# Second block's attention: a new order of the filling products, of VectorE's steps and of one PSUM ring

## The chip, the cores and the metric

One core of a Trainium2 chip runs the whole program as one launch. The metric is the device time of that launch in microseconds (us), as the median of three runs. A profiled execution of the same program gives the trace.

## What is computed

256 tokens of width 1024 pass two layers of a first block (mixer, memory attention, convolutional feed-forward) and then one layer of a second block. Only the first part of the second block is touched:

```python
xn = rmsnorm(x, norm_mix)
(u_rnn, u_gate, q, k_c, v_c, k_s, v_s, k_w, v_w, g_nsa, g_a, g_b) = jnp.split(xn @ w_in, cuts, axis=-1)
h_a = rg_lru(causal_depthwise_conv(u_rnn, conv_w, conv_b), gate_a_w, ..., lru_lambda)
y_a = h_a * jax.nn.gelu(u_gate, approximate=True)
y_b = nsa_mixer(q, k_c, v_c, k_s, v_s, k_w, v_w, g_nsa, ...)
merged = jax.nn.sigmoid(g_a) * (y_a @ proj_a) + jax.nn.sigmoid(g_b) * (y_b @ proj_b)
```

`rg_lru` is a gated linear recurrence on 1344 features: two block-diagonal gate products (4 blocks of 336), a tanh-built sigmoid of each, a decay `exp(...)`, and a scan over the tokens. `nsa_mixer` holds, for 16 heads of 64, attention over 15 compressed blocks, and two softmax attentions over the tokens (selected and window keys), each with a relative bias and a gate.

## The kernel before

**Products.** The weights arrive in one stream of pieces. A piece that is not "native" is split into a high and a low half: ScalarE casts the high half (`highs`, L991, the cast at L998), VectorE subtracts it for the low half (`lows_due`, L1499, at L1503), and TensorE adds three products (high-high, high-low, low-high) in `run` (L478). `features` (L484) makes one 128- or 112-column product of the layer's input over 8 row tiles: 24 matmuls of 256 columns. Native pieces are used as they come.

**The ring of pieces.** SyncE loads groups into a ring of NR = 4 places. Two neighbouring pieces of the same shape share a group, a native piece has one for itself (`grouped`, L176). A place is loaded again when TensorE has used the group four before. ScalarE and VectorE split up to LA = 3 pieces ahead of the one in hand, in the order of the stream, and wait for a piece that hasn't landed.

**PSUM.** Eight banks form two rings of four (L271): M for the streamed products, A for transposes, scores and attention values. `take` gives the next bank of a ring and waits for the engine that last emptied it.

**The stage around the change.** Twelve products `ur` (the recurrence's input, 112 features each), twelve `ug` (its gate, through `gelu_gate`, L812 and L1312, ScalarE's Gelu_apprx_tanh at L1315), and 24 small gate products (`lru`: three native matmuls each, recorded as six, then Tanh at L1377). After a `ur` product ScalarE copies it to `up`, and VectorE makes the depthwise convolution from four instructions (L2002, three times L2007). A decay step is Tanh, Exp and Square on ScalarE (L1349, L1351, L1353) and two VectorE instructions (L1987, L1991). In the order of TensorE's program: the twelve `ug` lie around the compression of keys and values (`phi`, its window sums `phi_sums` on VectorE, L1929, then `hid`, `cmp`), the transposes of queries and keys follow, and then the attention: for each of two query tiles i a compressed part (`csc`, `cpT`, `cpv`) and eight units un of four heads. Each unit issues scores (L947), the transposes of the unit before (L581), two steps of the list `lru_steps` as filling (`lru_next(2)`), and the values of the unit before (L934). Tile 0 has one block of 128 keys, tile 1 two. `lru_steps` (L437) is walked by TensorE, ScalarE and VectorE alike: 12 convolutions, 24 gate products, 3 decays; 38 of its 39 steps lie in the attention.

On VectorE a unit runs: copy of half the transposed probabilities (L2084, tile 1 only), maxima with the bias (L2069, L2072), after ScalarE's four exponentials (L1415) the reciprocals (L2075, L2077), then the two filling steps, then `finish`: the values of the unit before, scaled, out of PSUM (L2097). GpSimd adds them up (L2330). The attention's values lie in ring A, so that a unit of tile 1 takes five banks of a ring of four. After the attention the sixteen gate products `g2` follow, which need a Sqrt over the recurrence's factors first (L1437) on ScalarE and then Tanh (L1445).

Of the kernel before, what the change touches and what calls it, by code (L numbers as in the profile page):

```python
# [231 lines left out]
def build(nc, wstream, specs_out, cst_d, rel_d, par_d, par2_d, x_d, xT_d, memT_d, lnp_d, scr_d, out_d, layout):  # L232
    with ExitStack() as ctx:
# [230 lines left out]
        def tensor(e):  # L464
# [350 lines left out]
            for n in range(3):  # L815
                gelu_gate(n)
# [4 lines left out]
            gelu_gate(3)  # L821
            for c in range(2):
# [9 lines left out]
                gelu_gate(4 + 2 * c)  # L832
                gelu_gate(5 + 2 * c)
# [9 lines left out]
            for n in range(8, 12):  # L843
                gelu_gate(n)
# [17 lines left out]
            lru_todo = iter(lru_steps)  # L862

            def lru_next(n):
                for _ in range(n):
                    kind, m, *how = next(lru_todo, ("none", 0))
                    if kind == "conv":
                        features(("ur", m), W2, 8, 128, RW, span(UR + m * RP, RP), X, [], act, "ur", m)
                    if kind == "lru":
                        wi, jt = how  # L870
                        if jt == 0:
                            lru_w[:] = piece(("lru", m, wi), RP, 3, 336, (("GATE", ("gate_a_w_2", "gate_x_w_2")[wi], m), None, None),
                                             native=True)
                        x, (wW,) = lru_w
                        b = M.take(w, ("lru", m, wi, jt), act, "lru", m, wi, jt)
                        w.wait_ge(*landed(x))
                        w.wait_ge(vec, "xc", 3 * m + 2)
                        run(b[0:RP, 0:T], [(wW[:, k, jt * RP:(jt + 1) * RP], xc[0:RP, 3 * m + k, :]) for k in range(3)]
                            ).then_inc(*product.done("lru", m, wi, jt))
                        if jt == 2:  # L880
                            product.also("used", x)

            lru_w = [0, 0]
            for i in range(2):
# [102 lines left out]
        def scalar(e):  # L987
# [329 lines left out]
            for i in range(2):  # L1317
                for j in range(2):
                    w.wait_ge(act, "q2", j, i)
                    w.wait_ge(act, "kb", j, i)  # L1320
                if i:
                    w.wait_ge(vec, "qss", 0)
                e.activation(S[:, 0:1536], qb[:, i, :], ACT.Square).then_inc(*act.done("qsq", i))
                gelu_gate(i)
            gelu_gate(2)
            gelu_gate(3)
            for c in range(2):
                highs_of("phi", c)
                w.wait_ge(product, "phi", c)
                e.activation(ytmp[0:60, 256 * c:256 * c + 256], M["phi", c][0:60, 0:256],  # L1330
                             ACT.Gelu_apprx_tanh).then_inc(*act.done("phi", c))
                gelu_gate(4 + 2 * c)
                gelu_gate(5 + 2 * c)
                if c == 0:
                    w.wait_ge(cross, "cmp", 0)
                    e.activation(kc2[:, 0:64], A["cmp", 0][0:60, 0:64], ACT.Square, accum_out=kss).then_inc(*act.done("kss"))
            for n in range(8, 12):
                gelu_gate(n)
            for i in range(2):
                for h in range(2):  # L1340
                    w.wait_ge(cross, "q2T", i, h)
                    e.copy(q2[:, 4 * h:4 * h + 4, i * 128:(i + 1) * 128],
                           A["q2T", i, h][:, :].rearrange("p (k t) -> p k t", t=128)).then_inc(*act.done("q2T", i, h))

# [11 lines left out]
            for c in range(2):  # L1356
                for b in range(4):
                    w.wait_ge(stage_in[c][b])
            tmp_free = [(cross, "phT", 1)]
            lru_todo = iter(lru_steps)  # L1360

            def lru_next(n):
                for _ in range(n):
                    kind, m, *how = next(lru_todo, ("none", 0))
                    if kind == "conv":
# [17 lines left out]

            for i in range(2):
# [110 lines left out]
        def vector(e):  # L1495
# [420 lines left out]
            e.tensor_scalar(gq8, p2("qn"), 0.125, None, ALU.mult).then_inc(*vec.done("gq8"))  # L1916
            for i in range(2):
# [5 lines left out]
                lows_for("ug", i)  # L1923
            lows_for("ug", 2)
# [45 lines left out]
            for n in range(8, 12):  # L1970
                lows_for("ug", n)
# [10 lines left out]

            def decayed(m, n):
                tl, a2 = ytmp[0:RP, 0:256], ytmp[0:RP, 256:512]
                w.wait_ge(act, "lru", m // 3, 1, m % 3)
                w.wait_ge(vec, "xc", m)
                e.scalar_tensor_tensor(ia[0:RP, m, :], ia[0:RP, m, :], 1.0, xc[0:RP, m, :], ALU.add, ALU.mult).then_inc(*vec.done("ix", m))  # L1987
                w.wait_ge(act, "a2", m)
                w.wait_ge(vec, "ix", m)
                w.wait_ge(product, "lru", n, 1, 2)  # L1990
                e.scalar_tensor_tensor(xc[0:RP, m, :], a2, 1.0, tl, ALU.add, ALU.mult).then_inc(*vec.done("mult", m))  # L1991

            lru_todo = iter(lru_steps)

            def lru_next(n):
                for _ in range(n):
                    kind, m, *how = next(lru_todo, ("none", 0))
                    if kind == "conv":
                        lows_for("ur", m)
                        o = xc[0:RP, m, :]  # L2000
                        w.wait_ge(act, "ur", m)
                        e.tensor_scalar(o, up[0:RP, m, 3:259], cw2[:, m, 3:4], cb2[:, m:m + 1], ALU.mult,  # L2002
                                        ALU.add).then_inc(*vec.done("xc", m))
                        w.wait_ge(pool, "pad")
                        for k in range(3):
                            w.wait_ge(vec, "xc", m)
                            e.scalar_tensor_tensor(o, up[0:RP, m, k:k + T], cw2[:, m, k:k + 1], o, ALU.mult,  # L2007
                                                   ALU.add).then_inc(*vec.done("xc", m))
# [504 lines left out]
```

## Time and profile before

| | us |
|---|---|
| median of 3 runs (lowest, highest) | 1663.39 (1661.22, 1664.31) |
| profiled execution | 1660.03 |
| its span in the trace | 1658.2 |
| TensorE busy in the span | 1557.0 |
| VectorE, ScalarE, GpSimd busy | 1028.6, 800.3, 246.6 |
| from the first `ug` to the first score of tile 0 | 1109.9 to 1165.7 |
| attention, tile 0 | 1165.7 to 1242.3 |
| attention, tile 1 | 1242.3 to 1326.9 |
| four `g2` products | 1326.9 to 1339.5 |

Times within the trace count from the span's start. Busy time of TensorE includes the modelled end of each matmul, so that the time from one start to the next is the surer measure of what a piece of work takes. "Idle before" in a row of the timeline is the engine's wait before that row, and the arrow names who ended it.

### The profile page before, as it was taken

The page shows a single profiled execution, that of the slowest core. Times are in us where ns is not written, and L with a number is a line of the kernel's source. Part 1 is how long each engine was busy: PE and PEld are TensorE (multiplying, and loading weights), DVE is VectorE, ACT ScalarE, POOL GpSimd, SP SyncE. Part 2 cuts the span into 40 slices and gives each one's busy share as a digit, 9 for nine tenths or more (in the row PEclk, how much of TensorE's full clock was granted, in tenths as well). Part 3 has the DMA queues.
Part 4 walks back from the last instruction along what each step waited for, and adds up shares of the span by engine and source line. Part 5 has one row for each costly group of instructions (what it writes and reads, how often), then busy time and mean ns, then how long its engine had stood idle before and what let it go on. Part 6 is the DMA issues. An engine that isn't in the chain of part 4 may idle for free.

```text
span 1658.2 us, 25362 instructions
## 1 busy us (share of the span) xinstructions
PE 1557.0 (94%) x10403; PEld 1401.7 (85%) x10403; DVE 1028.6 (62%) x1704; ACT 800.3 (48%) x1435; POOL 246.6 (15%) x225
## 2 busy tenths in 40 slices
PE   8999999898998999989989999899988799989999
PEld 6899888798986889988789986697876699979987
DVE  5764585675855575577677865445655486646643
ACT  4545445364642455444356652453445564435532
POOL 2300131211202130032031101003010041100000
PEclk9999999899999999999999999899999899989999
DMA  8523355359554533255345555455211244535543
GB/s 314 222 102 115 103 216 174 119 178 218 190 208 152 203 123 111 88 190 181 128 160 190 182 192 176 152 184 187 90 45 48 77 153 148 202 107 189 188 178 127
DMA packets 41027, 261.33 MB, mean 158 GB/s; under 512 B 4512, under 2 KB 5152, under 8 KB 14672
## 3 DMA queue, kind: packets, MB, share of 16 engines
q1 hardware_dynamic: 35600, 238.44, 41.5%
q0 software_dynamic: 2944, 15.69, 3.7%
q10 hardware_dynamic: 2368, 5.58, 0.9%
q8 instruction: 82, 1.34, 0.3%
q14 instruction: 33, 0.27, 0.0%
HBM read 254.98 MB, written 4.19 MB: 156 GB/s over the span
## 4 chain that ended last, share of the span: by engine, by line
PE 75%; DVE 11%; ACT 5%; issue 3%; DMA 3%; POOL 2%; ACTq 0%; DVEq 0%; POOLq 0%; SPq 0%
PE ps L478 67%; PE ps L581 3%; DMA raw<-d_wst 2%; DVE lows L1503 2%; POOL sm L2189 1%; PE ps L662 1%; ACT wh L998 1%; ACT S L1415 1%; DVE ar L2007 1%; DVE sm L1536 1%; DVE xs L1533 1%; PE ps L683 1%; DVE S L2069 1%; PE ps L577 1%; PE ps L701 0%
## 5 line engine op out<-in xcount | busy, mean ns | idle before, releaser
L1503 DVE TENSOR_TENSOR lows<-raw,wh 128x1024 fp32r<-128x1024 f32 (+3 forms) x473 | 546.1, 1174 | 261.3 <-ACT wh L998 258.5
L478 PE MATMUL ps<-xTr,wh 128*128 128x256 f32 (+2 forms) x3664 | 674.1, 286 | 17.0 <-DVE S L1833 7.5
L478 PEld LDWEIGHTS ps<-xTr,wh 128*128 128x128 f32 (+2 forms) x3664 | 574.7, 192 | 22.3 <-issue 14.2
L998 ACT CAST wh<-raw 128x1024 fp32r<-128x1024 f32 (+3 forms) x473 | 455.6, 989 | 176.1 <-DMA raw<-d_wst 164.4
L478 PE MATMUL ps<-xTr,lows 128*128 128x256 f32 (+2 forms) x1832 | 522.0, 285 | 0.0
L478 PEld LDWEIGHTS ps<-xTr,lows 128*128 128x128 f32 (+2 forms) x1832 | 352.4, 192 | 0.0
L478 PE MATMUL ps<-wh,arR 128*128 128x512 f32 x928 | 296.4, 398 | 4.1 <-DVE ar L1653 4.1
L478 PEld LDWEIGHTS ps<-wh,arR 128*128 128x128 f32 x928 | 175.1, 189 | 48.1 <-DVE ar L1653 5.8
L478 PE MATMUL ps<-lows,arR 128*128 128x512 f32 x464 | 184.1, 397 | 0.0
L478 PE MATMUL ps<-arR,wh 128*128 128x256 f32 (+1 forms) x832 | 147.2, 280 | 2.2 <-DVE lows L1503 2.2
L478 PE MATMUL ps<-wh,xTr 128*128 128x512 f32 x384 | 125.0, 405 | 12.2 <-DVE xTr L1522 6.7
L478 PEld LDWEIGHTS ps<-arR,wh 128*128 128x128 f32 (+1 forms) x832 | 126.7, 188 | 2.8 <-issue 2.6
L478 PE MATMUL ps<-arR,lows 128*128 128x256 f32 (+1 forms) x416 | 116.0, 279 | 0.0
L478 PEld LDWEIGHTS ps<-lows,arR 128*128 128x128 f32 x464 | 87.6, 189 | 20.6
L478 PEld LDWEIGHTS ps<-wh,xTr 128*128 128x128 f32 x384 | 75.6, 197 | 30.8 <-DVE xTr L1522 7.1
L2189 POOL TENSOR_TENSOR sm<-sm,cst 128x1 f32<-128x1 f32 (+3 forms) x27 | 42.3, 1566 | 384.4 <-DVE sm L1541 235.5
L478 PEld LDWEIGHTS ps<-arR,lows 128*128 128x128 f32 (+1 forms) x416 | 78.2, 188 | 0.0
L478 PE MATMUL ps<-lows,xTr 128*128 128x512 f32 x192 | 77.5, 404 | 0.0
L2275 POOL TENSOR_TENSOR S<-S 128x256 f32<-128x256 f32 x44 | 42.0, 955 | 222.8 <-ACT S L1225 201.0
L1243 ACT ACTIVATE S<-ps,ar 128x256 f32<-128x256 f32 x88 | 49.4, 562 | 51.1 <-PE ps L478 51.1
L2263 POOL TENSOR_TENSOR ar<-ar 128x256 f32<-128x256 f32 x32 | 31.9, 998 | 233.3 <-DVE ar L1653 233.1
L1415 ACT ACTIVATE S<-S,sm 128x128 f32<-128x128 f32 (+1 forms) x64 | 28.3, 443 | 56.6 <-DVE sm L2072 56.5
(265 smaller groups left out, 1554.0 us busy)
## 6 DMA issues: line engine op xcount, KB each, us to landing
raw<-d_wst SPq DMA_DIRECT2D x196, 1024.0 KB, 4.8
raw<-d_wst SPq DMA_DIRECT2D x24, 512.0 KB, 3.5
raw<-d_wst SPq DMA_DIRECT2D x12, 896.0 KB, 4.6
raw<-d_wst SPq DMA_DIRECT2D x8, 672.0 KB, 4.6
ar<-d_lnp POOLq DMA_DIRECT2D x5, 1024.0 KB, 5.2
raw<-d_wst SPq DMA_DIRECT2D x8, 441.0 KB, 3.4
d_scr<-PT POOLq DMA_DIRECT2D x1, 3072.0 KB, 37.0
ar<-d_par POOLq DMA_DIRECT2D x2, 1192.0 KB, 9.6
```

Of the source, the lines that this page charges most:

```text
L478: op = e.matmul(out, s, m, start=start and i == 0, stop=stop and i == len(pairs) - 1)
L577: e.matmul(b[:, :], ident, cst("wmask"), start=True, stop=True)
L581: op = e.transpose(o, x, ident[0:x.shape[0], 0:x.shape[0]])
L662: op = e.matmul(b[:, h * 64:(h + 1) * 64], PTv[:, hold + h, k, :], va[:, k, v:v + 64], start=(k == 0), stop=(k == 1))
L683: op = e.matmul(bv[:, k, :], qT[br][lo:lo + 64, 2 * hh + k, i * 128:(i + 1) * 128], kT[br][lo:lo + 64, :], start=True, stop=True)
L998: e.copy(high_of(m), raw_of(m)).then_inc(*high.done(m))
L1243: e.activation(hc[:, s, :], M["up", l, m][:, 0:T], ACT.Identity, bias=cb[:, m:m + 1], scale=ck[:, m, 1:2]).then_inc(*act.done("h", l, m))
L1415: op = e.activation(Sv[:, hold + h, 0:nk], Sv[:, hold + h, 0:nk], ACT.Exp, bias=nb[:, h:h + 1], scale=1.0, accum_out=su[:, h:h + 1])
L1503: e.tensor_tensor(low_of(m), raw_of(m), high_of(m).bitcast(F32), ALU.subtract).then_inc(*low.done(m))
L2189: return e.tensor_tensor(dst, src, mhalf[0:p, 0:n], ALU.pow)
L2263: e.tensor_tensor(merged[:, d, :], merged[:, d, :], gates[:, gate_at[n] + d, :], ALU.add).then_inc(*pool.done("merged", l, n, d))
L2275: e.tensor_tensor(hc[:, s, :], hc[:, s, :], hc[:, s + 1, :], ALU.mult).then_inc(*pool.done("z", l, n))
```

## The change

- `lru_steps` now holds 51 steps: the twelve `ug` products are steps of it too. Six convolutions and three `ug` lie ahead of the attention where twelve `ug` lay. In tile 0 the other six convolutions alternate with gate products, in tile 1 nine `ug` alternate with gate products, one of each in a unit. The attention still takes 38 steps; four (one gate product with its decay, three decays) are left behind it, where one decay was.
- VectorE's convolution of step n is issued in step n + 1.
- VectorE's `finish(un - 1)` stands ahead of the two filling steps of unit un.
- The attention's values are written to ring M.
- Behind the attention ScalarE and VectorE split the pieces of the first `g2` products ahead of the steps that are left.
- GpSimd's clearing of `up`'s first columns stands ahead of the load of the bias table.

```diff
@@ lru_steps
-        lru_steps = [("conv", n) for n in range(RN)]
-        lru_steps += [("lru", n, wi, jt) for n in range(4) for wi in range(2) for jt in range(3)]
-        lru_steps += [("decay", 9 + k) for k in range(3)]
+        gate_steps = iter([("lru", n, wi, jt) for n in range(4) for wi in range(2) for jt in range(3)])
+        lru_steps = [("conv", 0), ("conv", 1), ("ug", 0), ("conv", 2), ("conv", 3), ("ug", 1), ("conv", 4), ("conv", 5), ("ug", 2)]
+        lru_steps += [("conv", 6), ("conv", 7)]
+        for n in range(8, RN):
+            lru_steps += [next(gate_steps), ("conv", n), next(gate_steps), next(gate_steps)]
+        lru_steps += [next(gate_steps)]
+        for n in range(3, RN):
+            lru_steps += [("ug", n), next(gate_steps)]
+        lru_steps += [*gate_steps, *(("decay", 9 + k) for k in range(3))]
@@ TensorE
-            for n in range(3):
-                gelu_gate(n)
...
+            lru_next(3)
             b = A.take(w, ("ng",), vec, "ng")
...
-            gelu_gate(3)
+            lru_next(1)
             for c in range(2):
...
-                gelu_gate(4 + 2 * c)
-                gelu_gate(5 + 2 * c)
+                lru_next(2)
...
-            for n in range(8, 12):
-                gelu_gate(n)
+            lru_next(1)
...
                 def finish(un):
-                    b = A.take(w, ("pv2", i, un), vec, "o2", i, un)
+                    b = M.take(w, ("pv2", i, un), vec, "o2", i, un)
@@ ScalarE (gelu_gate and lru_next as on TensorE)
+                    if kind == "ug":
+                        gelu_gate(m)
...
+            for n in range(3):
+                highs_of("g2", 0, n)
             lru_next(60)
@@ VectorE
+            def lru_next(n):
+                for _ in range(n):
+                    kind, m, *how = next(lru_todo, ("none", 0))
+                    if kind == "ug":
+                        lows_for("ug", m)
+                    if kind == "conv":
+                        lows_for("ur", m)
+                    if conv_due[0] is not None:
+                        convolved(conv_due[0])
+                    conv_due[0] = m if kind == "conv" else None
...
                 e.tensor_scalar(ve[i][:, 24:48], ve[i][:, 0:24], 1.0 / 64, 1e-6, ALU.mult, ALU.add).then_inc(*vec.done("qv", i))
-                lows_for("ug", i)
-            lows_for("ug", 2)
+                lru_next(1)
+            lru_next(1)
...
             phi_sums(0)
-            lows_for("ug", 3)
+            lru_next(1)
             q_scaled(0)
             for c in range(2):
                 lows_for("phi", c)
-                lows_for("ug", 4 + 2 * c)
+                lru_next(1)
                 if c == 0:
                     phi_sums(1)
-                lows_for("ug", 5 + 2 * c)
+                lru_next(1)
                 w.wait_ge(cross, "phT", c)
...
                     maxima(un)
-                    lru_next(2)
                     if un:
                         finish(un - 1)
+                    lru_next(2)
                 probs_copied(7)
+                finish(7)
                 lru_next(1)
-                finish(7)
...
+            for n in range(3):
+                lows_for("g2", 0, n)
             lru_next(60)
@@ GpSimd
             first_block_done()
+            e.memset(up[0:RP, :, 0:3], 0.0).then_inc(*pool.done("pad"))
...
-            e.memset(up[0:RP, :, 0:3], 0.0).then_inc(*pool.done("pad"))
```

## Rows read from the trace of the kernel before

**Rows 1.** Busy time by stage (length, engines, granted clock, DMA): tile 0, tile 1, then g2.

```profile
1165.69:1242.28 76.59, 67.60 (x527) 62.28 (x528) 48.69 (x165) 33.71 (x104) 5.82 (x8) 0.98 0.20 63
1242.28:1326.86 84.58, 67.64 (x397) 55.80 (x396) 39.62 (x140) 48.61 (x130) 5.82 (x8) 0.89 0.19 61
1326.86:1339.49 12.63, 12.63 (x97) 12.44 (x96) 7.17 (x12) 12.47 (x17) 0.74 (x1) 0.91 0.25 83
```

**Rows 2.** Waits of TensorE, both tiles: who ended them, us in total, times, longest.

```profile
PE ps L581 <- DVE ar L2097: 9.4, 5, 2.2
PE ps L934 <- DVE PT L2084: 4.5, 1, 4.5
```

**Rows 3.** Timeline of TensorE, tile 0: start, us, line, tiles, count, idle before.

```profile
1177.06 0.50 PE L478 MATMUL ps<-xTr,wh 128*112 128x256 f32 x2
...
1182.88 0.72 PE L947 MATMUL ps<-ar 64*128 64x128 f32 x8
1183.53 0.66 PE L581 MATMUL ps<-cst,S 128*128 128x128 f32 x4
...
1208.42 1.10 PE L934 MATMUL ps<-ar,PT 128*128 128x64 f32 x8 [0.79 <-DVE ar L2097]
...
1233.79 2.75 PE L478 MATMUL ps<-ar,raw 112*112 112x256 f32 x12
```

**Rows 4.** Timeline of TensorE, tile 1: one unit, then the end.

```profile
1259.15 2.00 PE L934 MATMUL ps<-ar,PT 128*128 128x64 f32 x16
1261.08 1.14 PE L947 MATMUL ps<-ar 64*128 64x256 f32 x8
1262.15 0.66 PE L581 MATMUL ps<-cst,S 128*128 128x128 f32 x4
1264.88 0.66 PE L581 MATMUL ps<-cst,S 128*128 128x128 f32 x4 [2.07 <-DVE ar L2097]
...
1319.86 3.64 PE L934 MATMUL ps<-ar,PT 128*128 128x64 f32 x16 [4.50 <-DVE PT L2084]
```

**Rows 5.** Timeline of ScalarE, one unit of tile 1.

```profile
1260.03 0.51 ACT L1415 ACTIVATE S<-S,sm 128x256 f32<-128x256 f32 x1 [1.83 <-DVE sm L2072]
...
1262.01 0.45 ACT L1377 ACTIVATE ar<-ps,sm 112x256 f32<-112x256 f32 x1
1262.36 0.59 ACT L1349 ACTIVATE ar<-ar,sm 112x256 f32<-112x256 f32 x1
...
1264.30 0.58 ACT L1404 COPY PT<-ps 128x512 f32<-128x512 f32 x1
```

**Rows 6.** Timeline of ScalarE: the first Gelu_apprx_tanh, and the first Exp after it.

```profile
1115.51 1.28 ACT L1315 ACT_TABLE_LOAD   x1
1116.81 0.39 ACT L1315 ACTIVATE ar<-ps 112x256 f32<-112x256 f32 x1
...
1169.44 1.28 ACT L1388 ACT_TABLE_LOAD   x1 [3.89 <-DVE S L2039]
```

**Rows 7.** The page's group of casts (count, busy, mean ns), and the loads of two pieces (KB, us to landing).

```profile
L998 ACT CAST wh<-raw 128x1024 fp32r<-128x1024 f32 (+3 forms) x473 | 455.6, 989 | 176.1 <-DMA raw<-d_wst 164.4
...
raw<-d_wst SPq DMA_DIRECT2D x2, 896.0 KB, 4.6
```

**Rows 8.** Timeline of VectorE: three quarters of a convolution, then copy and end of maxima.

```profile
1184.37 1.52 DVE L2007 SCALAR_TENSOR_TENSOR ar<-ar,par 112x256 f32<-112x256 f32 x3
...
1265.57 0.69 DVE L2084 COPY PT<-ps 128x512 f32<-128x512 f32 x1 [0.75 <-PE ps L581]
1267.67 0.17 DVE L2072 TENSOR_SCALAR sm<-sm 128x4 f32<-128x4 f32 x1
```

**Rows 9.** Timeline of TensorE at the first compression product.

```profile
1122.73 2.56 PE L478 MATMUL ps<-raw,S 128*60 128x256 f32 x11 [1.03 <-DVE S L1940]
```

**Rows 10.** Timeline of ScalarE behind the attention: Sqrt, first g2 Tanh.

```profile
1331.42 2.77 ACT L1437 ACTIVATE ar<-ar 112x3072 f32<-112x3072 f32 x1
...
1336.43 0.39 ACT L1445 ACTIVATE PT<-ps 128x256 f32<-128x256 f32 x1
```

More of the change, by code:

```diff
@@ L813, in gelu_gate @@
                 features(("ug", n), W2, 8, 128, RW, span(UG + n * RP, RP), X, [], act, "ug", n)
-            for n in range(3):
-                gelu_gate(n)
+            lru_w = [0, 0]
+            lru_todo = iter(lru_steps)
+            def lru_next(n):
[4 more added lines that the diff above has]
+                    if kind == "conv":
+                        features(("ur", m), W2, 8, 128, RW, span(UR + m * RP, RP), X, [], act, "ur", m)
+                    if kind == "lru":
+                        wi, jt = how
+                        if jt == 0:
+                            lru_w[:] = piece(("lru", m, wi), RP, 3, 336, (("GATE", ("gate_a_w_2", "gate_x_w_2")[wi], m), None, None),
+                                             native=True)
+                        x, (wW,) = lru_w
+                        b = M.take(w, ("lru", m, wi, jt), act, "lru", m, wi, jt)
+                        w.wait_ge(*landed(x))
+                        w.wait_ge(vec, "xc", 3 * m + 2)
+                        run(b[0:RP, 0:T], [(wW[:, k, jt * RP:(jt + 1) * RP], xc[0:RP, 3 * m + k, :]) for k in range(3)]
+                            ).then_inc(*product.done("lru", m, wi, jt))
+                        if jt == 2:
+                            product.also("used", x)
+            lru_next(3)
             b = A.take(w, ("ng",), vec, "ng")
@@ L860, in tensor @@
                        [qb[:, i, 1024 + k * 128:1024 + (k + 1) * 128] for k in range(4)])
[L862 to L883, printed above, removed]
             for i in range(2):
@@ L1315, in gelu_gate @@
                 e.activation(gg2[0:RP, n, :], M["ug", n][0:RP, 0:T], ACT.Gelu_apprx_tanh).then_inc(*act.done("ug", n))
[L1317 to L1343, printed above, removed]
             def decayed(m):
@@ L1354, in decayed @@
                 tmp_free[0] = (vec, "mult", m)
[L1356 to L1359, printed above, removed]
             lru_todo = iter(lru_steps)
@@ L1364, in lru_next @@
                     kind, m, *how = next(lru_todo, ("none", 0))
+                    if kind == "ug":
+                        gelu_gate(m)
                     if kind == "conv":
@@ L1382, in lru_next @@
                         decayed(m)
+            for i in range(2):
+                for j in range(2):
+                    w.wait_ge(act, "q2", j, i)
+                    w.wait_ge(act, "kb", j, i)
+                if i:
+                    w.wait_ge(vec, "qss", 0)
+                e.activation(S[:, 0:1536], qb[:, i, :], ACT.Square).then_inc(*act.done("qsq", i))
+                lru_next(1)
+            lru_next(2)
+            for c in range(2):
+                highs_of("phi", c)
+                w.wait_ge(product, "phi", c)
+                e.activation(ytmp[0:60, 256 * c:256 * c + 256], M["phi", c][0:60, 0:256],
+                             ACT.Gelu_apprx_tanh).then_inc(*act.done("phi", c))
+                lru_next(2)
+                if c == 0:
+                    w.wait_ge(cross, "cmp", 0)
+                    e.activation(kc2[:, 0:64], A["cmp", 0][0:60, 0:64], ACT.Square, accum_out=kss).then_inc(*act.done("kss"))
+            lru_next(1)
+            for i in range(2):
+                for h in range(2):
+                    w.wait_ge(cross, "q2T", i, h)
+                    e.copy(q2[:, 4 * h:4 * h + 4, i * 128:(i + 1) * 128],
+                           A["q2T", i, h][:, :].rearrange("p (k t) -> p k t", t=128)).then_inc(*act.done("q2T", i, h))
+            for c in range(2):
+                for b in range(4):
+                    w.wait_ge(stage_in[c][b])
+            tmp_free = [(cross, "phT", 1)]
             for i in range(2):
@@ L1969, in vector @@
                     q_scaled(1)
-            for n in range(8, 12):
-                lows_for("ug", n)
+            lru_next(1)
             w.wait_ge(cross, "kcT")
@@ L1981, in vector @@
                               A["k2T", i][:, :].rearrange("p (w f t) -> p w f t", w=2, t=128)).then_inc(*vec.done("k2T", i))
[L1983 to L2008, printed above, removed]
-                    if kind == "lru":
-                        wi, jt = how
-                        if jt == 0:
-                            lows_for("lru", m, wi)
-                        if late_at(m, wi, jt):
-                            decayed(late_of(m, wi, jt), m - 1)
-                    if kind == "decay":
-                        decayed(m, 3)
             for i in range(2):
```

39 lines of the change are left out of this document (38 added, 1 removed).

## Prediction

> **What bounds the kernel now.** The page comes first: TensorE is busy for 1557.0 of 1658.2 us, so most of the program has nothing to give, and what can be won lies where TensorE pauses. The busy time by stage shows where that is: in tile 0 it works 67.6 of 76.6 us, in tile 1 67.6 of 84.6, there at a mean granted clock of 0.89 [rows 1]. The waits name what it stands for. The largest sum is the transposes that wait for VectorE's `finish`, 9.4 us in five times, then the values at the end that wait for VectorE's copy, 4.5 [rows 2]. The timelines show how. In tile 1 a unit takes five banks of ring A; the second transpose needs the bank of the values two units back, and VectorE empties it only behind its filling steps [rows 4]. TensorE has little filling there: two gate products of 1.4 [rows 3]. In tile 0 filling is plenty, but the values wait 0.79 for the same `finish` [rows 3].
>
> **Unit prices.** Start to start, a big product (`ur` or `ug`) costs 2.9 us (two in 5.82), a gate product 1.3 to 1.4; in tile 0 scores 0.65, transposes some 0.4, values 1.0 [rows 3]; in tile 1 scores 1.07, transposes 0.9, values 1.9 [rows 4]. On ScalarE four exponentials cost 2.0, a Tanh 0.35, a decay 1.6 (1.94 with the next Tanh), a copy 0.6 [rows 5], a cast 0.9 [rows 7]. On VectorE copy and maxima take 2.3, a convolution 1.9 (its last three instructions are 1.52) [rows 8].
>
> **The work that moves.** No product is added or dropped. Ahead of the attention 12 `ug` become 9 products, so 3 x 2.9 = 8.7 us leave that stage. Tile 0 gives up 6 of 12 big products and gains 6 gate products: 17.4 - 7.8 = 9.6 leave it. Tile 1 has 9 big ones more and 7 gate products fewer, +17.0; one gate product (+1.3) falls behind the attention. The sum is nought; only pauses count.
>
> **Ahead of the attention.** VectorE now does two convolutions (3.8) before the window sums for which the first compression product waits; that product already waits 1.03 for them [rows 9]. One ScalarE table load fewer ahead of its second Square gives 0.6 back, so TensorE arrives at the same time and waits 4.3: +3.2. Likewise a convolution stands ahead of `hid` in both halves: +1.8 and +1.1. The last convolutions lie beside `ug` 2. From -8.7 this leaves **-2.4**; below that it can't fall under -8.7, above it reaches +1 if the pause lowers the clock.
>
> **Tile 0.** With `finish` ahead of the filling and the values in ring M, the waits for VectorE go. A unit with a convolution is 0.65 + 0.4 + 1.0 + 2.9 + 1.3 = 6.2 us of TensorE, one with two gate products 4.6. VectorE needs about 4.6 and 5.5 for the two, as the convolution is put off into the second: 10.1 beside 10.8, so TensorE sets the pace until unit 6. There the first decays come, and ScalarE, which splits ahead, stands for the load of the next `ug` pieces: 1.1 and 2.0 us of pauses. The last values wait 1.4 for a copy behind a decay, the final transposes 1.4 for GpSimd as before. Added up from the first score product: 61.8 instead of 76.6, **-14.8**; if VectorE stays late as now, only the moved 9.6.
>
> **Tile 1: what ScalarE pays.** TensorE's unit becomes 1.07 + 0.9 + 2.9 + 1.3 + 1.9 = 7.9 to 8.1. But each `ug` is a Gelu_apprx_tanh between exponentials. In the trace such a change of function has a table load in front: 1.28, and 1.30 from its start to the activation, on the way to Gelu, and another at the next Exp [rows 6]. Nine `ug` in tile 1 make 18 loads, 23.4 us of ScalarE. A unit is then 2.0 + 0.9 + 1.3 + 0.3 + 0.35 + 0.6 + 1.3 = 6.8 without and 8.4 with a decay, and behind a decay the next exponentials wait for VectorE's last decay instruction, copy and maxima (2.6 instead of the 0.6 of the copy beside it). Two units make 17.1 against TensorE's 15.8: ScalarE is what is late next. The rule of the Trainium skill, ScalarE: Activation LUTs, Table sets: the hidden batching unit, says to batch activations by table set, and speaks against this order; the trace has the 1.30 to price it. Its section What ACT_TABLE_LOAD costs adds a drain to 2.66 us a switch, which would put the sum some 20 us higher; the activation 0.02 behind the load shows no such drain [rows 6].
>
> **Tile 1: the loads of the weights.** `lru_steps` puts the pairs u6-u7, u9-u10 and the first `g2` pair four places of the ring behind a gate piece that TensorE finishes in the second filling step of units 0, 3 and 6. ScalarE splits the first of each pair in the first step of the same unit, so it waits there until that product is done and the load has landed, 4.6 us [rows 7]. Queued behind it are the Gelu, the Tanh and the copy for which the values wait. Walked through from the stage's start, the exponentials of units 0, 1, 3, 5, 7 begin at 13.4, 23.4, 40.5, 63.5 and 80.2. After the last come two casts, two loads, Gelu, Tanh, decay and copy, 9.2 to 9.7, and the values start at 89.9; from there to the end I take the old length, 1319.86 to 1326.86 = 7.0 [rows 1, 4]. That is 96.9 instead of 84.6: **+12.3**. Bounds: 82 if TensorE sets the pace; 105 if the clock falls as in [rows 1].
>
> **Behind the attention.** The first four `g2` products take the four banks of ring M; the fifth needs the first Tanh. Now that Tanh ends at 1336.8, 10.0 behind the end of tile 1, and the products take 12.6 [rows 1, 10]: nothing waits. Now three casts (2.8), a Tanh (0.4) and three more decays with VectorE's answer between them (6.5) stand ahead of Sqrt, less the cast that stood there: 18.4. TensorE has 1.3 + 12 of work: +**5.8** on its path, up to +8 with a low clock, 0 if the decays overlap.
>
> **Cheap edits.** GpSimd's clearing moves past one load on its own queue, and its cover is the 60 us until the first use; uncovered it would cost under 1 us. The bank of the values in ring M is emptied by `finish` a unit before it is needed: nothing. Were that late, the next product would wait.
>
> **Sum.** -2.4 - 14.8 + 12.3 + 5.8 = +0.9. The pauses of 4 to 5 us ahead of the first compression product and at the fifth `g2` product can lower the clock to 1.2 GHz for a few us, as the transition after the 4.50 wait did, where values take 3.64 instead of 1.9 [rows 4]: +1 to +2. I take +2. The profiled execution was 1660.0 and its span 1658.2, and 3.4 lies between it and the median 1663.4; the sum is made against the first, so the median comes to 1665.5.
>
> **Rivals.** *ScalarE isn't late* (faster). It waits 1.83 ahead of the exponentials in [rows 5]; if loads fall into such waits and the pieces land earlier, tile 1 goes at TensorE's 8 a unit and ends at about 82: 15 less, 1650.5. Against it: a load behind the last Gelu still stands ahead of a decay's Exp. Chance 0.31. *The clock* (slower). If each pause of 2 to 3 us in tile 1 is followed by a unit at 1.2 GHz, as 0.89 suggests [rows 1], a unit grows by up to 4; it decides once three units run at the lower level. Three such units, and 2 ahead of the attention: +14, 1678. Chance 0.20. *The change doesn't do what it says*: VectorE is still late for the maxima in tile 0, and only the 9.6 comes: +5, 1671. Chance 0.10. *The drain of the skill's page*: 1685, chance 0.02; no row bears it out.
>
> **How the numbers follow.** The forecast, -4 to +7 around 1665.5, has 0.37. A measurement of this kernel can tell about 0.2%, 3.3 us. Faster: 0.28 of the first rival and 0.06 of the forecast, 0.34. Same: 0.20 of the forecast, 0.03 each of the first rival and the third, 0.26. Slower: 0.11, 0.20, 0.07, 0.02, together 0.40. The range reaches from the first rival's 1650 to the clock's 1678.
>
> **What would show it.** Right: 18 loads more on ScalarE between the ends of tile 0 and tile 1, casts there that wait for a load of weights, tile 0 near 62 us with no transposes waiting for `finish`, a wait of some 4 us ahead of the fifth `g2` product. Wrong: ScalarE idle ahead of the exponentials of tile 1, units there at 8 us, or Gelu without loads.

## The result, and the profile after

The changed kernel takes 1680.97 us in the median of four runs (1677.73 to 1684.64), against 1663.36 in four runs before: a ratio of 1.0116, 95% interval 1.0095 to 1.0137. The forecast was 1665.5 with a range of 1649 to 1678, so the time lies above the range.

The profiled execution of the changed kernel took 1682.51 and its span is 1680.7, 22.5 longer than before. 5.3 of that lies in the first 1110 us, where both kernels do the same: the first `ur` product starts at 1115.13, and the first `ug` before at 1109.86. Over the profiled executions of this study that point lies anywhere between 1109.9 and 1115.5, so what follows compares stages and not ends. The busy time of the changed kernel by stage (length, then TensorE, its weight loads, VectorE, ScalarE, GpSimd, the granted clock, DMA share, GB/s): ahead of the attention, tile 0, tile 1, and to the fifth `g2` product.

```profile
1115.13:1174.52 59.39, 50.99 (x321) 41.20 (x320) 38.01 (x68) 19.67 (x32) 16.34 (x7) 0.89 0.38 128
1174.52:1238.27 63.75, 57.32 (x418) 51.33 (x419) 40.30 (x145) 37.17 (x111) 8.56 (x8) 0.98 0.25 80
1238.27:1342.71 104.44, 86.92 (x570) 77.47 (x570) 42.48 (x134) 68.53 (x137) 5.92 (x8) 0.88 0.19 66
1342.71:1361.61 18.90, 13.99 (x102) 13.13 (x101) 10.49 (x20) 16.98 (x24) 0.34 (x1) 0.86 0.50 167
```

Beside [rows 1], and 55.8 (1109.86 to 1165.69) for the first stage before: +3.6, -12.8, +19.9, +6.3. Where the change took work away (the first stage) it is longer, and the clock there is 0.89. The largest waits of TensorE over all four stages (engine, tile, line, who ended it: us in total, times, longest):

```profile
PE ps L939 <- DVE PT L2097: 10.9, 3, 5.6
PE ps L484 <- ACT PT L1451: 4.9, 1, 4.9
PE ps L484 <- DVE ar L2010: 4.1, 2, 2.7
PE ps L484 <- DVE S L1989: 3.9, 1, 3.9
```

The transposes that waited for `finish` [rows 2] are gone; all five of those waits lay in tile 1. In tile 0 of the kernel before only values waited for `finish`, 2.8 in three times, and they do no longer:

```profile
PE ps L934 <- DVE ar L2097: 2.8, 3, 1.3
```

In place of the transposes the values of tile 1 wait for VectorE's copy of the probabilities (L2097). Ahead of each of the three copies in VectorE's queue stands the last instruction of a decay (L1931), and that waits for ScalarE's Square (L1330), by 1.8, 3.5 and 1.7. The second of them:

```profile
1295.22 0.43 DVE L1931 SCALAR_TENSOR_TENSOR ar<-ar 112x256 f32<-112x256 f32 x1 [3.48 <-ACT ar L1330]
1295.57 0.68 DVE L2097 COPY PT<-ps 128x512 f32<-128x512 f32 x1
```

The fifth `g2` product waits for a Tanh, the compression for `hid` (L2010) and for the window sums (L1989). Those two waits, and two later places, in the timeline of TensorE:

```profile
1130.88 10.00 PE L484 MATMUL ps<-raw,S 128*60 128x256 f32 x32 [3.91 <-DVE S L1989]
...
1149.64 0.43 PE L484 MATMUL ps<-par,ar 128*60 128x64 f32 x4 [2.67 <-DVE ar L2010]
...
1238.27 3.51 PE L900 MATMUL ps<-ar 128*128 128x60 f32 x16
...
1335.71 3.65 PE L939 MATMUL ps<-ar,PT 128*128 128x64 f32 x16 [5.55 <-DVE PT L2097]
```

The first compression product takes 10.0 for its 32 matmuls, where at the full clock it takes 7.09 (shown under e8_short); the granted clock of that stretch is 0.71 of 2.4 GHz:

```profile
1130.88:1140.88 10.00, 10.00 (x33) 5.48 (x33) 9.16 (x16) 0.00 (x0) 3.41 (x3) 0.71 0.25 88
```

What stands ahead of the window sums is two convolutions on VectorE, 3.8 us, as forecast:

```profile
1124.92 0.41 DVE L1936 TENSOR_SCALAR ar<-ar,par 112x256 f32<-112x256 f32 x1
1125.43 1.53 DVE L1941 SCALAR_TENSOR_TENSOR ar<-ar,par 112x256 f32<-112x256 f32 x3
1126.88 0.41 DVE L1936 TENSOR_SCALAR ar<-ar,par 112x256 f32<-112x256 f32 x1
1127.32 1.53 DVE L1941 SCALAR_TENSOR_TENSOR ar<-ar,par 112x256 f32<-112x256 f32 x3
...
1128.93 1.80 DVE L1989 TENSOR_TENSOR S<-PT,par 128x120 f32<-128x120 f32 x8
```

And tile 1 on ScalarE, unit 0: the exponentials start, then a cast waits 3.25 for weights that haven't landed, and around the Gelu stand two loads of tables, 1.28 each:

```profile
1254.97 0.51 ACT L1419 ACTIVATE S<-S,sm 128x256 f32<-128x256 f32 x1 [3.27 <-DVE sm L2085]
...
1260.30 0.94 ACT L1003 CAST wh<-raw 128x896 fp32r<-128x896 f32 x1 [3.25 <-DMA raw<-d_wst]
1261.25 1.28 ACT L1320 ACT_TABLE_LOAD   x1
1262.55 0.38 ACT L1320 ACTIVATE ar<-ps 112x256 f32<-112x256 f32 x1
...
1263.79 1.28 ACT L1419 ACT_TABLE_LOAD   x1
1265.08 0.51 ACT L1419 ACTIVATE S<-S,sm 128x256 f32<-128x256 f32 x1
```

Over tile 1 the groups by line count 9, 5 and 4 loads, the 18 of the forecast, and the waits of ScalarE hold the three landings:

```profile
L1320 ACT ACT_TABLE_LOAD x9 | 11.5, 1283 | 0.2
L1328 ACT ACT_TABLE_LOAD x5 | 6.4, 1283 | 0.1
L1419 ACT ACT_TABLE_LOAD x4 | 5.1, 1283 | 0.1
```
```profile
ACT wh L1003 <- DMA raw<-d_wst: 10.0, 3, 4.4
```

### The profile page after: what moved, and what is told of

It reads as the page before. It is cut to its first block and busy times, and to the rows that moved or that the text cites. A ratio compares the mean times of both kernels' runs of the same rounds, so it can differ in the third digit from the quotient of the medians.

```text
span 1680.7 us, 25388 instructions
## 1 busy us (share of the span) xinstructions
PE 1571.1 (93%) x10403; PEld 1414.7 (84%) x10403; DVE 1032.0 (61%) x1704; ACT 825.0 (49%) x1453; POOL 248.3 (15%) x225
## 5 line engine op out<-in xcount | busy, mean ns | idle before, releaser
L484 PEld LDWEIGHTS ps<-xTr,wh 128*128 128x128 f32 (+2 forms) x3664 | 580.2, 194 | 27.3 <-issue 14.5
L1839 DVE SCALAR_TENSOR_TENSOR S<-ps,ar,S 128x255 f32<-128x255 f32 x88 | 42.1, 479 | 11.6 <-ACT S L1248 11.6
```

The costliest lines, as they stand in the source:

```text
L484: op = e.matmul(out, s, m, start=start and i == 0, stop=stop and i == len(pairs) - 1)
L1839: e.scalar_tensor_tensor(h[:, 1:T], b[:, 0:T - 1], ck[:, m, 0:1], h[:, 1:T], ALU.mult, ALU.add).then_inc(*vec.done("conv0", l, m))
```

## Experiments

All start from the changed kernel. The theories: **P**, a pause of TensorE costs itself and the low clock behind it; **T**, the loads of tables set tile 1; **L**, so do the waits for landing weights; **B**, the decays left behind the attention hold up the first Tanh of `g2`. The table has the medians, the ratio to the kernel before with its interval, and the stages of the profiled execution: ahead (first 112-column product to first score product of the compressed part), tile 0 (to the same product of tile 1), tile 1 (to the first `g2` product) and behind (to the end). By these bounds tile 1 holds the last gate product too: 84.2 before, 106.4 after. The ratio is to the kernel before as it was run again beside each (medians 1660.7 to 1662.1), not to the first row's median. The changed kernel was not run again, so a difference of under 3 between two medians is not clear of this. The stages are those of one execution each: that of e8_short is the fastest of its seven, that of e4_mixed the slowest of its ten.

| kernel | median | ratio (95%) | ahead | tile 0 | tile 1 | behind |
|---|---|---|---|---|---|---|
| before | 1663.4 | | 55.8 | 76.6 | 84.2 | 331.7 |
| changed | 1681.0 | 1.0116 (1.0095 to 1.0137) | 59.4 | 63.8 | 106.4 | 336.0 |
| e1_tanh | 1666.9 | 1.0032 (1.0014 to 1.0051) | 59.3 | 63.8 | 91.9 | 336.7 |
| e2_conv_late | 1669.6 | 1.0049 (1.0034 to 1.0065) | 48.7 | 63.8 | 106.4 | 336.0 |
| e3_dummies | 1679.7 | 1.0121 (1.0101 to 1.0141) | 59.3 | 64.1 | 106.1 | 337.5 |
| e4_mixed | 1666.6 | 1.0028 (1.0014 to 1.0041) | 55.7 | 75.2 | 94.3 | 330.6 |
| e5_far2 | 1670.9 | 1.0053 (1.0036 to 1.0069) | 59.0 | 63.0 | 94.8 | 337.8 |
| e6_tail | 1678.8 | 1.0109 (1.0091 to 1.0127) | 59.0 | 63.8 | 106.6 | 335.5 |
| e7_batch | 1650.2 | 0.9930 (0.9911 to 0.9949) | 48.5 | 64.4 | 85.3 | 336.7 |
| e8_short | 1670.5 | 1.0046 (1.0029 to 1.0062) | 54.8 | 65.7 | 97.9 | 334.5 |
| e9_filled | 1639.9 | 0.9866 (0.9848 to 0.9883) | 48.4 | 62.2 | 79.6 | 334.3 |
| e10_ring_a | 1684.5 | 1.0137 (1.0120 to 1.0154) | 59.4 | 63.8 | 109.6 | 336.1 |
| e11_finish_late | 1680.7 | 1.0109 (1.0094 to 1.0124) | 59.6 | 63.5 | 107.2 | 336.6 |
| e12_both_undone | 1690.7 | 1.0174 (1.0158 to 1.0190) | 59.3 | 63.7 | 118.2 | 335.8 |

**The loads of tables (e1_tanh).**

```diff
-                e.activation(gg2[0:RP, n, :], M["ug", n][0:RP, 0:T], ACT.Gelu_apprx_tanh).then_inc(*act.done("ug", n))
+                e.activation(gg2[0:RP, n, :], M["ug", n][0:RP, 0:T], ACT.Gelu_apprx_tanh if n < 3 else ACT.Tanh).then_inc(*act.done("ug", n))
```

> The changed kernel with Tanh in place of Gelu_apprx_tanh in the nine `ug` steps of tile 1: a part of the computation is changed, so that ScalarE changes no function table there. Theory T (tables): 18 loads, 23 us of ScalarE, go away; the waits for landing weights (3.3, 4.4 and 2.4 us) stay; the other units go at TensorE's 8.0, and tile 1 falls from 104.2 to about 88, the whole from 1681 to about 1665. Rival W (weights): tile 1 is set by the landing of pieces in the ring, and the loads lie in those waits; tile 1 stays above 99, the whole above 1676. Rival C (clock alone): TensorE's clock sets the length, and tile 1 moves by under 3.

Tile 1 falls by 14.5 and nothing else moves. That is less than the 23.0 of the 18 loads. The rest shows in ScalarE's waits for the maxima ahead of its exponentials in tile 1, here in e1_tanh and then in the changed kernel: some 8 of the loads had lain in these.

```profile
ACT S L1419 <- DVE sm L2085: 19.6, 8, 3.3
```
```profile
ACT S L1419 <- DVE sm L2085: 11.6, 6, 3.3
```

The waits for landings stay in e1_tanh, so they are a cause of their own:

```profile
ACT wh L1003 <- DMA raw<-d_wst: 11.8, 3, 4.5
```

**The convolutions behind the window sums (e2_conv_late).** VectorE collects the convolutions of the six `ur` ahead of the attention in a list and makes them up later.

```diff
+                    if ahead[0]:
+                        put_off.extend([m] if kind == "conv" else [])
...
                 if c == 0:
                     phi_sums(1)
+                    made_up(2)
...
                     q_scaled(1)
+                    made_up(1)
             lru_next(1)
+            made_up(3)
+            ahead[0] = False
```

> The changed kernel, with VectorE's convolutions 0 to 5 moved behind the window sums: two behind the second sums, one behind the queries' scaling, three behind the last `ug` ahead of the attention. Theory P (the pauses pull the clock down): TensorE's waits ahead of the first compression product and the two small products fall from 3.9, 2.7 and 1.4 to 1.0, 0.8 and 0.4, the granted clock there rises from 0.7 to 1.0, and the stage falls from 59.4 to about 47.5, 6 of it from the waits and 6 from the clock: the whole comes to about 1669. Rival D (the waits only): the clock stays low for another reason, and 6 come back: 1675. Rival E: the convolutions now stand ahead of the masks and maxima at the start of tile 0, and what is won there is lost again: 1678 or more.

The stage falls by 10.7, to 48.7. The waits are 0.7 for the sums and 1.1 for `hid`, and the granted clock of the stage is 1.00, against 0.89:

```profile
PE ps L484 <- DVE ar L2019: 1.1, 2, 0.8
PE ps L484 <- DVE S L1997: 0.7, 1, 0.7
```
```profile
1112.29:1161.02 48.73, 45.05 (x321) 37.62 (x320) 37.78 (x68) 19.86 (x33) 14.46 (x7) 1.00 0.46 155
```

The waits named fell from 8.0 to 1.8, by 6.2, and a new one of 1.5 came at the transposes behind. The other 6 are clock. Rival D is out, and so is E: tile 0 didn't move.

**The clock by itself (e3_dummies, e8_short).** Only dummy products are added, so that TensorE is busy in its pauses.

```diff
+                if c == 0:
+                    warm(8)                      # e8_short: 4
                 for a in (0, 8):
...
+                if i:
+                    warm(12)                     # e8_short: 6
                 finish(7)
+                if not i:
+                    warm(4)                      # e8_short: 2
...
+                    if (v, n) == (0, 4):
+                        warm(11)                 # e8_short: 5
```

> The changed kernel with dummy products of TensorE in four of its pauses, each no longer than the pause: 8 ahead of the first compression product, 4 ahead of tile 0's last transposes, 12 ahead of tile 1's last values, 11 ahead of the fifth `g2` product. They work on constants and nothing reads them. Theory P: the waits' ends don't move, but the clock behind them stays at 2.4 GHz: first compression products 10.0 to 7.1, start of tile 1 (scores and `ug`) 8.2 to 4.7, last values 3.65 to 1.9; the whole falls by 7 to 11, to 1670 to 1674. Rival D: the clock is low for another reason, and the time stays at 1681 or rises by what the dummies outlast their pauses.

> The changed kernel with dummy products on TensorE in the same four pauses, but 4, 2, 6 and 5 of them, since each took 0.87 to 0.9 and the 8, 4, 12 and 11 outlasted their pauses (7.0 against 3.9 ahead of the first compression product). Theory P: they end inside the pauses, the clock behind stays at 2.4 GHz, and what the longer row gave back and lost at once is now kept: 2.9 at the first compression products, 3.5 at the start of tile 1, 1.8 at the last values: the whole falls by 6 to 9, to 1672 to 1675. Rival D: with dummies that leave a rest of the pause the clock falls all the same: 1679 or more.

e3_dummies misses its 1670 to 1674. I had taken a dummy at 0.44, from a row of such products with ten records; but each leaves two, and costs 0.87 to 0.9. With the eight of e3_dummies the first compression product starts 2.9 later after the start of its stage (18.7 instead of 15.8); it takes 7.12 instead of 10.0 and gives back the same 2.9. So the time of e3_dummies doesn't change, though its clock does:

```profile
1122.33 7.03 PE L583 MATMUL ps<-cst 128*128 128x512 f32 x16
1129.30 7.12 PE L484 MATMUL ps<-raw,S 128*60 128x256 f32 x32
```

With half of them the pause ends within 0.3 of where it did and the products behind are as fast. In e8_short, the same place and the start of tile 1:

```profile
1122.21 3.60 PE L583 MATMUL ps<-cst 128*128 128x512 f32 x8
1126.55 7.09 PE L484 MATMUL ps<-raw,S 128*60 128x256 f32 x32 [0.74 <-DVE S L1997]
...
1226.36 3.73 PE L583 MATMUL ps<-cst 128*128 128x512 f32 x4
...
1231.06 1.89 PE L902 MATMUL ps<-ar 128*128 128x60 f32 x16
```

The scores of the compressed part take 1.89 there instead of 3.51. Work that nobody reads makes the kernel 10.5 faster in the median (1681.0 to 1670.5). In the profiled execution the stages give 4.6 ahead, 8.5 in tile 1 and 1.5 behind, less 2.0 in tile 0. There the clock had already fallen in this execution: the two dummies take 3.73, about twice the price, and outlast their pause. Theory P holds, and this is what the low clock behind four pauses costs, less what the dummies cost themselves.

**Landing weights (e5_far2).**

```diff
-                highs_of("ug", n)
+                highs_of("ug", n, far=LA if n < 3 else 2)
-                            highs_of("lru", m, wi)
+                            highs_of("lru", m, wi, far=LA if m < 2 else 2)
```

and the same for VectorE's `lows_for`.

> The changed kernel, with ScalarE and VectorE splitting only two pieces ahead instead of three in tile 1, so that no piece is split in the step that frees its place. The loads of tables stay. Theory L (landing): ScalarE's waits of 3.3, 4.4 and 2.4 for weights go, tile 1 falls from 106.4 (first score product to first `g2`) to about 97, the whole to about 1671. Rival T2: the loads of tables alone set tile 1 and the waits had lain in ScalarE's slack: 103 or more, 1677 or more. Rival S: split later, the pieces are late for TensorE, which then waits for the low halves: no gain.

No wait for a DMA is left among ScalarE's in tile 1, and the stage falls by 11.6; a single wait of 1.4 of TensorE for low halves is what rival S brings. T and L are both true. The largest waits of ScalarE there are now those for VectorE's maxima and for the last transposes:

```profile
ACT S L1419 <- DVE sm L2085: 11.1, 5, 3.3
ACT arR L1432 <- PE ps L587: 6.8, 2, 6.5
```

**Another deal (e4_mixed).** The twelve `ug` stand ahead of the attention as before (the last `lru_next(1)` there is `lru_next(4)` on all three engines); c is an `ur`, g a gate product:

```diff
+        lru_steps = [("ug", n) for n in range(RN)]
+        for c in "cccc" "gcggcgggcgggcg" "g" "cg" "cgggcgcggggggg" "g":
+            lru_steps.append(next(conv_steps if c == "c" else gate_steps))
+        lru_steps += [("decay", 9 + k) for k in range(3)]
```

> Another deal of the same steps with the changed kernel's other edits: all twelve `ug` ahead of the attention as in the kernel before, eight `ur` and 11 gate products in tile 0, four `ur` and 13 gate products in tile 1, each gate product at least a unit behind the convolutions it needs; no Gelu and no convolution where it hurt. Theory T with P: ahead of the attention as before, 55.8; tile 0 and tile 1 together about 143 instead of 161 (before) and 168 (changed); two decays less behind the attention than in the changed kernel: the whole 1645 to 1650, faster than both. Rival V (the new places of `finish` and of the values give little, and tile 0 was shorter because products were taken out of it): 1658 or more.

At 1666.6 it is 17 slower than the upper end I expected and lies in rival V's range. That the new places of `finish` and of the values give little, as V has it, is shown below for tile 0 of the changed kernel's deal (e12_both_undone), not for this one. Tile 0 with its eight `ur` came to 75.2, and tile 1 to 94.3. The largest single piece is L again. In the step of the last `ur` ScalarE splits a `g2` piece whose place is only freed a unit later; it waits 8.39, VectorE's last convolution behind it, and a gate product 9.22 for that; the 14.5 behind this wait have a granted clock of 0.58. Two rows, of ScalarE and of TensorE:

```profile
1293.13 1.04 ACT L1001 CAST wh<-raw 128x1024 fp32r<-128x1024 f32 x1 [8.39 <-DMA raw<-d_wst]
```
```profile
1297.46 1.17 PE L482 MATMUL ps<-ar,raw 112*112 112x256 f32 x2 [9.22 <-DVE ar L1939]
```

So a deal without Gelu in the attention has the same trap; how this one does with two pieces ahead stays open.

**Behind the attention (e6_tail).**

```diff
-            lru_next(60)
...
+            lru_next(1)
+            for n in range(3):
+                g2_tanh(0, n)
+                lru_next(1)
```

> The changed kernel; on ScalarE the Tanh of the first three `g2` products stand between the four decays left behind the attention, ahead of Sqrt, instead of behind it. Theory B (behind the attention): the wait of 4.9 ahead of the fifth `g2` product goes, and with it 1 to 2 of low clock: the whole falls by 5 to 7, to about 1675. Rival R: Sqrt comes 1 to 2 later, the recurrence behind it is the next thing late, and the time stays at 1679 to 1683.

A miss: 2 instead of 5 to 7, and the 2 are not clear of the noise; the time is next to rival R's 1679, for another reason than rival R's. The wait for the Tanh is gone, but ScalarE, still at its decays and Sqrt, doesn't split the next pieces either, and a later `g2` product waits for them:

```profile
1360.47 0.77 PE L484 MATMUL ps<-xTr,wh 128*128 128x256 f32 x2 [3.60 <-DVE lows L1517]
```

**The parts together (e7_batch, e9_filled).** e7_batch joins e2_conv_late, e5_far2 and e6_tail, and takes the Gelu out of the attention without changing what is computed:

```diff
+                if n < 3:
+                    e.activation(gg2[0:RP, n, :], M["ug", n][0:RP, 0:T], ACT.Gelu_apprx_tanh).then_inc(*act.done("ug", n))
+                else:
+                    e.copy(gg2[0:RP, n, :], M["ug", n][0:RP, 0:T]).then_inc(*act.done("ugc", n))
...
             e.activation(qall, qall, ACT.Sqrt).then_inc(*act.done("sqrt"))
...
+            e.activation(gall, gall, ACT.Gelu_apprx_tanh).then_inc(*act.done("ug", 3))
```

> The changed kernel with four edits together: the convolutions behind the window sums (as measured: 10.7 less), the `ug` of the attention copied out of PSUM by ScalarE's Copy and nine of them given Gelu_apprx_tanh in one instruction behind Sqrt (no loads of tables in tile 1), two pieces ahead in tile 1, and the first `g2` Tanh between the decays. If the causes are what the theories T, P, L and B say they add up: 10.7 + 14.5 + 6 to 9 + 5 less than 1681, that is 1642 to 1645, faster than both kernels. Rival V: TensorE's 8 us a unit bind first, so that T and L don't add: 1650. Rival W: one more cause is hidden behind these: 1658 or more.

It is the first that beats the kernel before, but at rival V's 1650. T and L together give 21.1 in tile 1 and not 26.1: TensorE binds there first, as its units follow each other without a wait up to the last values, 7.96 from one set of scores to the next. The batch of Gelu was not run alone; with two pieces ahead tile 1 was 94.8 (e5_far2), and with the batch besides it is 85.3. And B's 5 don't come, as in e6_tail: a later `g2` product waits 4.6 for low halves. Two scores and the values between them, and TensorE's waits for low halves:

```profile
1253.46 1.14 PE L952 MATMUL ps<-ar 64*128 64x256 f32 x8
...
1259.59 1.90 PE L939 MATMUL ps<-ar,PT 128*128 128x64 f32 x16
1261.42 0.93 PE L952 MATMUL ps<-ar 64*128 64x256 f32 x6
```
```profile
PE ps L484 <- DVE lows L1525: 5.0, 2, 4.6
```

e9_filled adds to e7_batch what e6_tail, e7_batch and e8_short taught (`lows_for` on VectorE goes the same way as `highs_of`):

```diff
                 g2_tanh(0, n)
+                highs_of("g2", 0, n + 3)
...
+                if not i:
+                    warm(2)
                 probs_turned(7)
                 lru_next(1)
+                if i:
+                    warm(3)
                 finish(7)
+                warm(1)
```

> The four edits of the earlier run of this name's kind (convolutions late, Copy with Gelu in one batch, two pieces ahead, Tanh between the decays), and two more: ScalarE and VectorE split one more piece of `g2` behind each of those Tanh, and dummy products (0.87 each) stand in the pauses at the ends of the tiles: 2 and 1 in tile 0, 3 and 1 in tile 1. Theories B and P: the wait of 4.6 for low halves ahead of the seventh `g2` product goes, and the start of tile 1 (scores and `ug`, 8.1) goes at 2.4 GHz (4.7): 7 to 9 less than 1650, that is 1641 to 1643. Rival R: the recurrence or the weights behind take it back: 1647 or more.

1639.9, 1.3% under the kernel before, with a granted clock of 1.00 in all three stages. What the dummies and what the earlier splitting bring of the 10.3 from e7_batch was not run apart; the stages give 5.7 in tile 1, 2.2 in tile 0 and 2.4 behind.

```profile
1110.53:1158.94 48.41, 45.06 (x321) 37.64 (x320) 37.99 (x68) 19.63 (x32) 14.43 (x7) 1.00 0.46 156
1158.94:1221.12 62.18, 59.20 (x424) 51.34 (x425) 39.30 (x144) 35.98 (x110) 7.79 (x8) 1.00 0.25 82
1221.12:1300.71 79.59, 78.97 (x585) 69.88 (x583) 43.80 (x135) 45.61 (x122) 9.19 (x8) 1.00 0.24 87
```

**`finish` and the ring (e10_ring_a, e11_finish_late, e12_both_undone).**

```diff
-                    b = M.take(w, ("pv2", i, un), vec, "o2", i, un)      # e10, e12
+                    b = A.take(w, ("pv2", i, un), vec, "o2", i, un)
...
-                    if un:                                              # e11, e12
-                        finish(un - 1)
                     lru_next(2)
+                    if un:
+                        finish(un - 1)
```

> The changed kernel with the attention's values written to ring A again. Theory F (`finish` ahead of the filling is enough): tile 0, which needs four banks of ring A a unit, stays at 63.8; in tile 1, with five, the transposes wait for `finish` of the unit before, which comes later than the last exponentials only where VectorE is late: 0 to 3 more, the whole 1681 to 1684. Rival M (the ring is what freed the transposes): tile 0 rises by 4 to 6.

> The changed kernel with VectorE's `finish` behind the two filling steps again, the values in ring M. Theory F: in tile 0 the values' bank in ring M comes round again after three filling products, before `finish` has emptied it, and the filling waits: tile 0 rises by 3 to 6. Theory M (the ring alone is enough): tile 0 stays within 1 of 63.8; tile 1, set by ScalarE, doesn't move in either.

> The changed kernel with both undone: values in ring A and `finish` behind the filling steps, as in the kernel before; only the deal of the products stays. By the prediction's sum tile 0's 12.8 less is 9.6 of products moved out of it and the rest waits for `finish`: tile 0 comes to about 67, the transposes wait for `finish` again. Rival N: the waits in the kernel before came from twelve convolutions on VectorE, and with half of them and `put off` they don't come back: tile 0 stays at 64.

Tile 0 is 63.5 to 63.8 in all three: neither edit, nor both, does anything there. Rival N holds: with six convolutions on VectorE instead of twelve, each put off by a step, `finish` is in time in either order. Which of the two, the number or the putting off, does it was not run. So the rise of 3 to 6 that theory F expected of e11_finish_late doesn't come, nor the 67 of e12_both_undone. In tile 1 the stage is 3.2 longer without the ring, 0.8 without the order, and 11.8 longer without both: one edit, either, does most of the work. Without both the transposes wait for `finish` as in [rows 2, 4]:

```profile
PE ps L587 <- DVE ar L2110: 21.4, 5, 7.7
```

## Why the prediction was wrong

**The step that failed is the clock's: the +2 in the sum, and the cap of +1 ahead of the attention.** The stages without the clock were put at +0.9; measured they add up to +16.9. Some 11 of these 16 lie where the trace shows a low granted clock, 6.2 ahead of the attention and about 5 in tile 1. The terms that the prediction worked out as waits nearly fit.

- **Ahead of the attention**, -2.4 forecast, +3.6 measured. The rise of the three waits was put at 3.2, 1.8 and 1.1 and is 2.9, 1.9 and 1.1; the work moved out is the forecast's 8.7. What failed is that the cap of +1 for a low clock was far too small. Start to start the first compression product takes 9.9 instead of 7.0, the second 8.7 instead of 7.0, the last `ug` 4.6 instead of 2.9: 6.2 in all. e2_conv_late won back 6.2 of waits and 6 of clock.
- **Tile 0**, -14.8 forecast, -12.8 measured. The size was nearly right and the reason wrong: 9.6 of products left, but the rest is not `finish` and the ring, as I put it. With both undone the stage is as short, so the rest comes with the convolutions, half as many and each put off (e12_both_undone).
- **Tile 1**, +12.3 forecast, +19.9 measured. The mechanism was right in each part: 18 loads, casts that wait in units 0, 3 and 6 (3.3, 4.4, 2.4), ScalarE ahead of TensorE as the bound. By e1_tanh the loads are worth 14.5, by e5_far2 the landings 11.6, each taken alone. The exponentials of units 0, 1, 3, 5, 7 were put at 13.4, 23.4, 40.5, 63.5 and 80.2 from the stage's start and begin at 16.7, 26.8, 44.6, 68.4 and 87.4. 3.3 is there at the first: scores and `ug` at the start run at low clock behind the pauses at the end of tile 0. With dummies in that pause the first exponentials begin at 13.1 (e8_short). Another 1.6 comes up to unit 5, behind the pauses ahead of the values, at granted clocks like the first one below; that this is the clock is read from the trace and was not run. The last 2.3, between units 5 and 7, are no clock, as the second shows: there ScalarE is later than walked, with the landing of 2.4 in unit 6. Dummies take 8.5 off this stage, but some 3.6 of that lies at its end, where the kernel before had the low clock as well [rows 4].

```profile
1297.86:1306.62 8.76, 8.76 (x49) 7.79 (x49) 5.56 (x15) 7.53 (x15) 0.72 (x1) 0.65 0.00 1
1306.62:1325.64 19.02, 17.81 (x137) 16.11 (x136) 7.71 (x29) 14.29 (x30) 1.57 (x2) 1.00 0.44 151
```

- **Behind**, +5.8 forecast, +6.3 measured, the wait of 4.9 where it was put. But its remedy on ScalarE showed that the splitting of pieces is queued there too.

Three sums of the prediction don't come out, by too little to matter: the terms ahead of the attention make -2.6 and not -2.4, those behind it 18.8 and not 18.4, and 1660.0 with 2.9 and 3.4 is 1666.3 and not 1665.5.

The **rival of the clock** was the true case, with its 0.20: +14 and 1678, 3 under the measured median. That its number is so near is in part luck: it had 2 ahead of the attention, where 6.2 came, and three units of tile 1 at up to 4 each, where the start and two later units cost about 5. I had the rows for it, 3.64 instead of 1.9 behind a wait [rows 4] and a stage at 0.89 [rows 1], and forecast pauses of 4.3 ahead of the attention, 1.1 to 2.0 in tile 0 and 4 to 5 behind, yet charged the clock for two of them and only 2 us. The signs of being right all came (18 loads, casts that wait, tile 0 at 63.8, 4.9 ahead of the fifth `g2` product), but they would have come with the rival too; and no transposes waited for `finish` in tile 0 even before, so that this one could show nothing.

The first rival had a point: ScalarE's waits ahead of its exponentials stayed in tile 1, and some 8 of the 23 of loads fell into them (e1_tanh). The other 14.5 made the stage longer.

Of the rule to batch by table set (the Trainium skill, ScalarE: Activation LUTs, Table sets: the hidden batching unit) the runs say that it holds here: one batch of nine instead of nine Gelus between exponentials takes tile 1 from 94.8 to 85.3 (e5_far2 to e7_batch, whose other two edits left tile 1 as it was in e2_conv_late and e6_tail). The drain of which the Trainium skill tells (ScalarE: Activation LUTs, What ACT_TABLE_LOAD costs) doesn't show in the changed kernel either: the Gelu at 1262.55 starts 0.02 behind its load, and the load 0.01 behind the cast.

## What to carry to other kernels

When a change makes TensorE wait, charge the wait and then what runs behind it at the lower clock: here the second was as large as the first ahead of the attention (6.2 and 5.9), and dummy products that end inside the pauses are a cheap way to measure it. A filling product brings all its work along: its evacuation with that function's table on ScalarE, and the splitting of a piece several places on, which stands still if that place isn't free. So walk the ring for every deal before you choose one, and copy out of PSUM what needs a foreign table, to apply the function in one batch.

## What the runs showed of the hardware

A dummy product of 512 columns in full precision took 0.87 to 0.9 us, and 1.87 at the end of tile 0 in e8_short, where the clock was low already. With four of them in a wait that ended 0.74 later the next product took 7.09 instead of 10.0, with nothing ahead of it changed. A load of a table took 1.28, and the activation behind it started 0.02 later. I had not expected that idle work could bring 0.6% of a whole kernel. The first 1110 us of the program, where the kernels do the same, differed by up to 5.7 us between executions, more than several of the effects above, and only the stages could be compared that finely.
